# Two of the token norms of a three-layer kernel: one sum over tokens in place of eight, and the third weight unit worked beside the first two

## The chip, the cores and the metric

One core of one Trainium2 chip. The metric is the device time of one execution, in microseconds (us); lower is better. The kernel is one program that runs three transformer layers one after another.

## The reference, cut to what matters

There are 512 tokens (`SEQ`) of width 1024 (`D_MODEL`), in float32. Every sublayer adds a normed result to the residual, and the next sublayer takes a normed copy of that residual:

```python
def rmsnorm(x, gain):
    x32 = x.astype(jnp.float32)
    y = x32 * lax.rsqrt(jnp.mean(x32 * x32, axis=-1, keepdims=True) + RMS_EPS)
    return (y * gain.astype(jnp.float32)).astype(x.dtype)

        h = memory_cross_attention(rmsnorm(x, norm_cross_pre[l]), rmsnorm(mem, mem_norm[l]), ...)
        x = x + rmsnorm(h, norm_cross_post[l])
        h = conv_glu_ffn(rmsnorm(x, norm_ffn_pre[l]), w_ffn_in[l], ffn_conv_w[l], ffn_conv_b[l], w_ffn_out[l])
        x = x + rmsnorm(h, norm_ffn_post[l])

def conv_glu_ffn(xn, w_up, conv_w, conv_b, w_down):
    gu = xn @ w_up
    gate, up = jnp.split(gu, 2, axis=-1)
    gate = causal_dwconv(gate, conv_w) + conv_b.astype(gate.dtype)
    return (jax.nn.silu(gate) * up) @ w_down
```

At two places a post-norm, an addition to `x` and a pre-norm stand back to back: after the cross attention (`norm_cross_post`, then `norm_ffn_pre` ahead of the gated FFN), and after that FFN (`norm_ffn_post`, then `attn_norm_e_2` ahead of the projections of the next layer's attention). These are the double norms of this case.

## The kernel before, in words

**Layout.** Activations lie feature-major: 1024 features are 8 blocks (`KT`) of 128 partitions, with 512 tokens along the free axis. A weight *unit* is a 128x1024 slice of a weight matrix: all 8 feature blocks for 128 output features. All 339 units of the kernel are one stream in `w_in`.

**Products in three passes.** Each float32 operand is split into a high and a low part (`wh`, `wl`; `xh`, `xl`), and a product is `wh*xh + wh*xl + wl*xh`. So one unit costs TensorE (PE) 8 blocks x 3 = 24 matmuls of 128x512, which add up in one PSUM bank.

**The weight ring.** Four buffers (`RING`). SyncE (SP) loads unit k into `raw` once unit k-4 is done (`unit_done`); ScalarE (ACT) rounds it into `wh` in `raise_to`, in its own program order (`high_split`); GpSimd (POOL) then makes `wl = raw - wh` in `lower`, in two halves of 128x512 (`unit_split`). VectorE (DVE) takes finished PSUM banks away and counts them in `emptied`.

**A double norm.** The pre-norm's factor 1/rms of a token is applied to the *results* of the products, so PE can begin on `x*gain` before that factor is known. DVE (`normed_twice`) makes for each block b: `scale` (tmp = y*gain*factor, the factor read from PSUM), `accumulate` (x += tmp), and for the block before it `low` (xl = x*gain - xh). ACT (`prepare`) makes for each block xh = x*gain, and its square into one of two `sq` buffers, which it may fill again when PE has used it. PE (`early_units`) works two units (n0 and n0+1) side by side in this block loop: for block kt four high products (`wh*xh`, `wl*xh` of both units), and for the block before it `low_product`: first `token_sums` of its squares, then `wh*xl` of both units. `token_sums` sums the squares over features as 4 matmuls with 4 columns each, which the trace shows as 8. After the loop come units n0+2 and n0+3 whole (`piece`), into the two `score_ps` banks.

**What follows the sum.** ACT takes the square root (L1511), DVE the reciprocal (L2118), PE spreads it over the partitions (`spread_tokens`, 4 transposes, L758; after two blocks of n0+2), and DVE copies it into `rstd` (L2159). Only then can DVE empty unit n0 and the ones behind it.

**After the first double norm** (n0 = `fup0`), units come in pairs of gate (even) and up (odd) blocks. DVE's `gated` makes for a pair: the gate emptied and scaled (L2090), a convolution of three instructions (L2391, L2097), after ACT's SiLU the product with the up bank (L2610), the factor again (L2611) and the split into high and low (L2101, L2102). ACT's `gated` raises units up to n0+2i+4 ahead of the SiLU of pair i. Units n0+4 and n0+5 (`next_unit`) go to the `gemm_ps` banks of n0 and n0+1 once these are emptied; from n0+6 on (`units`) each unit waits until the unit two before it is emptied:

```python
                        for n in range(first, first + RING):
                            pe.wait_ge(unit_split, RING * i + (n + 1))
                            pe.wait_ge(emptied, RING * i + (n - 1))
```

**After the second double norm** (n0 = `even_in`), ACT waits until unit n0 is emptied, squares it for the head norms (L1976), and only then raises unit n0+4; PE does `query_stat(0)`, then `next_unit(n0+4)`.

Queues are strictly in program order on each engine. The order around the change is written out by hand; no planner sets it.

Of the kernel before, what the change touches and what calls it, by code (L numbers as in the profile page):

```python
# [31 lines left out]
D = 1024  # L32
KT = D // P
# [151 lines left out]
def build(nc, x_in, mem_in, w_in, par_in, con_in, moba_in, alibi_in, na_in, dist_in, out):  # L185
    with ExitStack() as ctx:
# [200 lines left out]
        def early_bank(n0, n):  # L387

            return score_ps[:, n - n0 - 2, :] if n - n0 in (2, 3) else gemm_ps[:, n % 2, :]
# [179 lines left out]
        def _(pe):  # L569
# [109 lines left out]
            def early_units(n0, highs):  # L679


                keep_clock(2)
                pe.wait_ge(unit_split, n0 + 2)
                pe.wait_ge(emptied, n0)
                both = [(n, early_bank(n0, n)) for n in (n0, n0 + 1)]

                def low_product(kt):
                    take(square_ready)
                    token_sums(sq[:, kt % 2, :], kt == 0, kt == KT - 1).then_inc(square_used, 1)
                    pe.wait_ge(rhs_ready, blocks_split[0] + kt + 1)  # L690
                    for n, o in both:
                        m = pe.matmul(o, wh[:, n % RING, kt * P:(kt + 1) * P], xl[:, kt, :], start=False,
                                      stop=(kt == KT - 1))
                        if kt == KT - 1:
                            m.then_inc(unit_done, 1)

                for kt in range(KT):
                    w = slice(kt * P, (kt + 1) * P)
                    pe.wait_ge(high_made, highs + kt + 1)
                    for n, o in both:  # L700
                        pe.matmul(o, wh[:, n % RING, w], xh[:, kt, :], start=(kt == 0), stop=False)
                        pe.matmul(o, wl[:, n % RING, w], xh[:, kt, :], start=False, stop=False)
                    if kt:
                        low_product(kt - 1)
                low_product(KT - 1)
                blocks_split[0] += KT
                for n in (n0 + 2, n0 + 3):
                    pe.wait_ge(unit_split, n + 1)
                    piece(n, early_bank(n0, n), 0, 2, xh, xl)
                    if n == n0 + 2:  # L710
                        spread_tokens()
                    piece(n, early_bank(n0, n), 2, KT, xh, xl)

            def next_unit(n, h, l):

# [756 lines left out]
        def _(act):  # L1472
# [17 lines left out]
            def raise_to(n):  # L1490

                while raised[0] <= min(n, UNITS - 1):
# [4 lines left out]
                    act.activation(wh[:, k % RING, :], raw[:, k % RING, :], ACT.Copy).then_inc(high_split, 1)  # L1497
                    raised[0] += 1

            def prepare(src, gain, h, ready=None, adds=0, tokens=False, banks={}):  # L1500


                base = taken.get(square_added, 0)
                act.activation(eps[:, 3:4], eps[:, 0:1], ACT.Sqrt)
                for b in range(KT):
                    high_and_square(src, gain, h, b, ready, base=base if adds else None, bank=banks.get(b))
                if adds:
                    taken[square_added] = base + adds
                if tokens:
                    take(square_used, 2)  # L1510
                    act.activation(token_std, turn_ps[:, 0, 0:T], ACT.Sqrt, bias=eps[:, 0:1],  # L1511
                                   scale=1.0 / D).then_inc(std_ready, 1)
                else:
                    finish_norm(rstd[:, :])
# [428 lines left out]
            def crossed(b):  # L1943
# [5 lines left out]
                else:  # L1949
# [2 lines left out]
            last = (FIRST["co"] + U_CO - 1) % 2  # L1952
            prepare(y, None, None, crossed, adds=KT - 3, tokens=True,
                    banks={KT - 2: score_ps[:, last, :], KT - 1: gemm_ps[:, last, :]})
            prepare(x, "norm_ffn_pre", xh, lambda b: take(block_ready), tokens=True)
            raise_to(FIRST["fup0"] + 3)
            gated()

            act.wait_ge(emptied, FIRST["fdown1"] + KT)
# [6 lines left out]
                    table_piece(arena[:, (23 + b) * N:(24 + b) * N], alibi_in[:, b * N:(b + 1) * N])  # L1966

            prepare(y, None, None, stored_and_loaded, adds=KT - 2, tokens=True)
            prepare(x, "attn_norm_e_2", xh, lambda b: take(block_ready), tokens=True)
            even, even_out = FIRST["even_in"], FIRST["even_out"]  # L1970
            raise_to(even + 3)
            for b in range(5):
                act.wait_ge(emptied, even + b + 1)
                if b >= 2:
# [94 lines left out]
        def _(dve):  # L2069
# [58 lines left out]
            def normed_twice(post, pre):  # L2128


                inverse_tokens()
                added = taken.get(block_ready, 0)
                made = []

                def scale(b):
                    if b >= 2:
                        dve.wait_ge(block_ready, added + b - 1)
                    sent_stt(tmp[:, b % 2, :], y[:, b, :], p_(post, b), spread_rstd, ALU.mult, ALU.mult)
                    made.append(taken[dve_step])

                def accumulate(b):
                    dve.wait_ge(dve_step, made[b])
                    sent(dve.tensor_tensor(x[:, b, :], x[:, b, :], tmp[:, b % 2, :], ALU.add), block_ready)

                scale(0)
                accumulate(0)
                scale(1)
                for b in range(1, KT):
                    if b + 1 < KT:
                        scale(b + 1)  # L2150
                    accumulate(b)
                    low(x, pre, xh, xl, b - 1)
                low(x, pre, xh, xl, KT - 1)
                inverse_spread()

            def inverse_spread():
# [806 lines left out]
```

## Time and profile before

| | |
|---|---|
| time, median of 3 runs | 2170.78 us (2170.11 to 2171.26) |
| span of the profiled execution (first to last instruction) | 2169.7 us |
| PE busy | 2149.4 us (99%), 10303 matmuls |
| DVE / ACT / POOL busy | 983.0 / 847.1 / 893.9 us (45 / 39 / 41%) |
| first double norm, from its first product to the end of unit n0+3 | 409.62 to 440.24 us of the span |
| second double norm, the same | 784.54 to 815.16 us |

The profiled execution has no device time of its own beside its span. The median of the runs is 1.1 us above that span, the work that lies around it. Times below are positions in the span. A matmul's own duration (some 390 ns) overlaps its neighbours' because the engine is pipelined; the distance from start to start is what it costs.

### The profile page before, as it was taken

The numbers are of one execution on the slowest core, as the hardware profiler recorded it, in microseconds if no ns is written. First come the engines' busy times: TensorE is split into PE (matmuls) and PEld (weight loads), VectorE is DVE, ScalarE is ACT, GpSimd is POOL, SyncE is SP. The second block draws the span as 40 slices with busy tenths as digits, with TensorE's granted clock in tenths as the row PEclk, the third lists the DMA queues.
The fourth block names the chain that finished last, engine by engine and source line by source line (L and its number), as shares of the span: only waits on it lengthen the run. The fifth ranks groups of instructions, "written<-read, shape, count | busy, mean of one in ns | idle before, by whom it ended". The sixth has DMA issues, their size and how long they took to land.

```text
span 2169.7 us, 27420 instructions
## 1 busy us (share of the span) xinstructions
PE 2149.4 (99%) x10303; PEld 1731.4 (80%) x10303; DVE 983.0 (45%) x1496; ACT 847.1 (39%) x1282; POOL 893.9 (41%) x684
## 2 busy tenths in 40 slices
PE   9999999999999999999999999999999999999999
PEld 7875787788888877767888888888888878888887
DVE  5755645576626143465432231346534655313221
ACT  6435645422222243565433232444333434423221
POOL 5431254154444443213444444433343315444443
PEclk9999999999999999999999999999999999999999
DMA  4222132133322332102222222322222213222223
GB/s 175 78 68 69 57 99 78 59 102 122 106 97 97 110 113 88 50 30 69 97 97 97 97 97 97 106 81 75 78 87 78 72 44 109 97 97 97 97 97 97
DMA packets 55109, 193.24 MB, mean 89 GB/s; under 512 B 6112, under 2 KB 6368, under 8 KB 54752
## 3 DMA queue, kind: packets, MB, share of 16 engines
q1 hardware_dynamic: 50112, 180.41, 25.0%
q10 hardware_dynamic: 4896, 11.41, 1.6%
q8 instruction: 73, 1.20, 0.2%
q14 instruction: 28, 0.23, 0.0%
HBM read 189.69 MB, written 2.10 MB: 88 GB/s over the span
## 4 chain that ended last, share of the span: by engine, by line
issue 52%; POOL 29%; PE 17%; POOLq 1%; DMA 0%; DVE 0%; ACT 0%; SPq 0%; ACTq 0%
POOL wl L552 29%; PE gemm_ps L587 6%; PE gemm_ps L588 6%; PE gemm_ps L589 6%; POOLq L549 0%; POOLq L561 0%; DMA x<-x_in 0%; DVE xl L2090 0%; ACT xh L1892 0%; ACT wh L1497 0%; PE turn_ps L729 0%; DVE x L2236 0%; SPq L526 0%; ACTq L1891 0%
## 5 line engine op out<-in xcount | busy, mean ns | idle before, releaser
L552 POOL TENSOR_TENSOR wl<-raw,wh 128x512 fp32r<-128x512 f32 x678 | 890.1, 1335 | 1258.0 <-ACT wh L1497 1248.8
L1497 ACT ACTIVATE wh<-raw 128x1024 fp32r<-128x1024 f32 x339 | 358.7, 1059 | 752.7 <-DMA raw<-w_in 742.1
L587 PE MATMUL gemm_ps<-xh,wh 128*128 128x512 f32 x1176 | 465.8, 396 | 0.0
L589 PE MATMUL gemm_ps<-xh,wl 128*128 128x512 f32 x1176 | 459.0, 390 | 0.0
L588 PE MATMUL gemm_ps<-xl,wh 128*128 128x512 f32 x1176 | 458.8, 390 | 0.0
L588 PE MATMUL gemm_ps<-arena_r,wh 128*128 128x512 f32 (+1 forms) x1088 | 417.0, 383 | 0.0
L587 PE MATMUL gemm_ps<-arena_r,wh 128*128 128x512 f32 (+1 forms) x832 | 320.0, 385 | 1.2 <-POOL wl L552 0.7
L589 PE MATMUL gemm_ps<-arena_r,wl 128*128 128x512 f32 (+1 forms) x832 | 317.4, 381 | 0.0
L587 PEld LDWEIGHTS gemm_ps<-xh,wh 128*128 128x128 f32 x1176 | 221.5, 188 | 49.6 <-issue 2.3
L588 PEld LDWEIGHTS gemm_ps<-xl,wh 128*128 128x128 f32 x1176 | 221.5, 188 | 47.4 <-issue 2.2
L589 PEld LDWEIGHTS gemm_ps<-xh,wl 128*128 128x128 f32 x1176 | 221.3, 188 | 46.7
L588 PEld LDWEIGHTS gemm_ps<-arena_r,wh 128*128 128x128 f32 x1088 | 205.0, 188 | 41.2 <-issue 1.4
L2090 DVE SCALAR_TENSOR_TENSOR arena<-gemm_ps,rstd 128x512 f32<-128x512 f32 (+1 forms) x116 | 84.7, 731 | 261.9 <-PE gemm_ps L589 211.1
L2236 DVE TENSOR_TENSOR x<-x,gemm_ps 128x512 f32<-128x512 f32 x84 | 57.6, 686 | 316.8 <-PE gemm_ps L589 305.1
L587 PEld LDWEIGHTS gemm_ps<-arena_r,wh 128*128 128x128 f32 x832 | 157.0, 189 | 33.7 <-issue 2.4
L589 PEld LDWEIGHTS gemm_ps<-arena_r,wl 128*128 128x128 f32 x832 | 156.9, 189 | 30.1
L2097 DVE SCALAR_TENSOR_TENSOR tmp<-gemm_ps,rstd 128x512 f32<-128x512 f32 x64 | 44.2, 691 | 207.9 <-PE gemm_ps L589 207.9
L587 PE MATMUL gemm_ps<-y_r,wh 128*128 128x512 f32 x256 | 100.0, 391 | 0.0
L589 PE MATMUL gemm_ps<-y_r,wl 128*128 128x512 f32 x256 | 99.6, 389 | 0.0
L2586 DVE TENSOR_TENSOR arena_r<-sq,arena_r 128x512 fp32r<-128x512 f32 x64 | 93.7, 1464 | 2.2
L621 PE MATMUL gemm_ps<-xh,wh 128*128 128x512 f32 x216 | 88.5, 410 | 1.3 <-DVE xl L2308 0.5
L623 PE MATMUL gemm_ps<-xh,wl 128*128 128x512 f32 x216 | 84.6, 392 | 0.0
(429 smaller groups left out, 2548.6 us busy)
## 6 DMA issues: line engine op xcount, KB each, us to landing
raw<-w_in SPq DMA_DIRECT2D x338, 512.0 KB, 3.4
arena<-na_in ACTq DMA_DIRECT2D x14, 256.0 KB, 2.7
out<-x ACTq DMA_DIRECT2D x8, 256.0 KB, 2.9
x<-x_in SPq DMA_DIRECT2D x6, 256.0 KB, 6.5
arena<-alibi_in ACTq DMA_DIRECT2D x6, 256.0 KB, 3.5
arena<-moba_in ACTq DMA_DIRECT2D x1, 1024.0 KB, 4.8
arena<-mem_in ACTq DMA_DIRECT2D x1, 1024.0 KB, 5.6
arena<-dist_in ACTq DMA_DIRECT2D x1, 896.0 KB, 4.5
```

The lines of the kernel that those rows point to most:

```text
L552: m = pool.tensor_tensor(wl[:, k, half], raw[:, k, half], wh[:, k, half].bitcast(F32), ALU.subtract)
L587: pe.matmul(o, wh[:, n % RING, w], h[:, kt, 0:width], start=(kt == 0), stop=False)
L588: pe.matmul(o, wh[:, n % RING, w], l[:, kt, 0:width], start=False, stop=False)
L589: last = pe.matmul(o, wl[:, n % RING, w], h[:, kt, 0:width], start=False, stop=(kt == nkt - 1))
L621: pe.matmul(o, wh[:, n % RING, w], h[:, kt, :], start=(kt == 0), stop=False)
L623: m = pe.matmul(o, wl[:, n % RING, w], h[:, kt, :], start=False, stop=(kt == KT - 1))
L1497: act.activation(wh[:, k % RING, :], raw[:, k % RING, :], ACT.Copy).then_inc(high_split, 1)
L2090: sent(dve.scalar_tensor_tensor(out=o, in0=a, scalar=scalar, in1=b, op0=op0, op1=op1), s)
L2097: done(dve.scalar_tensor_tensor(out=o, in0=a, scalar=scalar, in1=b, op0=op0, op1=op1), s)
L2236: sent(dve.tensor_tensor(x[:, e, :], x[:, e, :], bank(n0, e), ALU.add), emptied)
L2586: done(dve.tensor_tensor(l[:, b, :], sq[:, b % 2, :], h[:, b, :].bitcast(F32), ALU.subtract), rhs_ready)
```

## The change

- The eight `token_sums` of the block loop go. ACT writes the squares of the pre-norm into the 8 blocks of `y` (free by then), in the new `prepare_into`, without waiting for anyone to use them. DVE adds them up into `square_sum` in seven additions (`sum_square`), the first ahead of the last `low`, six behind it. PE makes one `whole_token_sums` from that.
- Unit n0+2 trails in the block loop: from kt = 2 on, its three products of block kt-2. What is left of it (two blocks) and unit n0+3 follow; the token sums stand after 3 blocks of n0+3, the spread after 6.
- ACT raises unit n0+3 before the block loop, not after the norm.

```diff
--- before.py
+++ after.py
@@ -685,8 +685,6 @@
                 both = [(n, early_bank(n0, n)) for n in (n0, n0 + 1)]
 
                 def low_product(kt):
-                    take(square_ready)
-                    token_sums(sq[:, kt % 2, :], kt == 0, kt == KT - 1).then_inc(square_used, 1)
                     pe.wait_ge(rhs_ready, blocks_split[0] + kt + 1)
                     for n, o in both:
                         m = pe.matmul(o, wh[:, n % RING, kt * P:(kt + 1) * P], xl[:, kt, :], start=False,
@@ -702,14 +700,20 @@
                         pe.matmul(o, wl[:, n % RING, w], xh[:, kt, :], start=False, stop=False)
                     if kt:
                         low_product(kt - 1)
+                    if kt == 2:
+                        pe.wait_ge(unit_split, n0 + 3)
+                    if kt >= 2:
+                        piece(n0 + 2, early_bank(n0, n0 + 2), kt - 2, kt - 1, xh, xl)
                 low_product(KT - 1)
                 blocks_split[0] += KT
-                for n in (n0 + 2, n0 + 3):
-                    pe.wait_ge(unit_split, n + 1)
-                    piece(n, early_bank(n0, n), 0, 2, xh, xl)
-                    if n == n0 + 2:
-                        spread_tokens()
-                    piece(n, early_bank(n0, n), 2, KT, xh, xl)
+                piece(n0 + 2, early_bank(n0, n0 + 2), KT - 2, KT, xh, xl)
+                pe.wait_ge(unit_split, n0 + 4)
+                piece(n0 + 3, early_bank(n0, n0 + 3), 0, 3, xh, xl)
+                whole_token_sums()
+                taken[square_made] = taken.get(square_made, 0) + KT
+                piece(n0 + 3, early_bank(n0, n0 + 3), 3, 6, xh, xl)
+                spread_tokens()
+                piece(n0 + 3, early_bank(n0, n0 + 3), 6, KT, xh, xl)
 
             def next_unit(n, h, l):
 
@@ -1496,6 +1500,19 @@
                         act.wait_ge(unit_done, k + 1 - RING)
                     act.activation(wh[:, k % RING, :], raw[:, k % RING, :], ACT.Copy).then_inc(high_split, 1)
                     raised[0] += 1
+
+            def prepare_into(gain, squares, n0):
+
+                act.activation(eps[:, 3:4], eps[:, 0:1], ACT.Sqrt)
+                raise_to(n0 + 3)
+                for b in range(KT):
+                    take(block_ready)
+                    act.activation(xh[:, b, :], x[:, b, :], ACT.Copy, scale=p_(gain, b)).then_inc(high_made, 1)
+                    act.activation(squares[:, b, :], x[:, b, :], ACT.Square).then_inc(square_made, 1)
+                taken[square_added] = taken.get(square_added, 0) + KT - 1
+                take(square_used, 2)
+                act.activation(token_std, turn_ps[:, 0, 0:T], ACT.Sqrt, bias=eps[:, 0:1],
+                               scale=1.0 / D).then_inc(std_ready, 1)
 
             def prepare(src, gain, h, ready=None, adds=0, tokens=False, banks={}):
 
@@ -1952,8 +1969,7 @@
             last = (FIRST["co"] + U_CO - 1) % 2
             prepare(y, None, None, crossed, adds=KT - 3, tokens=True,
                     banks={KT - 2: score_ps[:, last, :], KT - 1: gemm_ps[:, last, :]})
-            prepare(x, "norm_ffn_pre", xh, lambda b: take(block_ready), tokens=True)
-            raise_to(FIRST["fup0"] + 3)
+            prepare_into("norm_ffn_pre", y, FIRST["fup0"])
             gated()
 
             act.wait_ge(emptied, FIRST["fdown1"] + KT)
@@ -1966,9 +1982,8 @@
                     table_piece(arena[:, (23 + b) * N:(24 + b) * N], alibi_in[:, b * N:(b + 1) * N])
 
             prepare(y, None, None, stored_and_loaded, adds=KT - 2, tokens=True)
-            prepare(x, "attn_norm_e_2", xh, lambda b: take(block_ready), tokens=True)
+            prepare_into("attn_norm_e_2", y, FIRST["even_in"])
             even, even_out = FIRST["even_in"], FIRST["even_out"]
-            raise_to(even + 3)
             for b in range(5):
                 act.wait_ge(emptied, even + b + 1)
                 if b >= 2:
@@ -2142,6 +2157,13 @@
                     dve.wait_ge(dve_step, made[b])
                     sent(dve.tensor_tensor(x[:, b, :], x[:, b, :], tmp[:, b % 2, :], ALU.add), block_ready)
 
+                def sum_square(b):
+                    take(square_made, 2 if b == 1 else 1)
+                    if b > 1:
+                        landed(square_added)
+                    sent(dve.tensor_tensor(square_sum, y[:, 0, :] if b == 1 else square_sum, y[:, b, :], ALU.add),
+                         square_added)
+
                 scale(0)
                 accumulate(0)
                 scale(1)
@@ -2150,7 +2172,10 @@
                         scale(b + 1)
                     accumulate(b)
                     low(x, pre, xh, xl, b - 1)
+                sum_square(1)
                 low(x, pre, xh, xl, KT - 1)
+                for b in range(2, KT):
+                    sum_square(b)
                 inverse_spread()
 
             def inverse_spread():
```

## Rows read from the trace of the kernel before

**Rows 1.** The page, busy time of each engine.
```profile
PE 2149.4 (99%) x10303; PEld 1731.4 (80%) x10303; DVE 983.0 (45%) x1496; ACT 847.1 (39%) x1282; POOL 893.9 (41%) x684
```

**Rows 2.** Timeline of PE, first double norm: start us, us, instruction, count.
```profile
414.76 0.95 PE L740 MATMUL turn_ps<-con,sq 128*128 128x4 f32 x8
415.56 0.71 PE L692 MATMUL gemm_ps<-xl,wh 128*128 128x512 f32 x2
...
417.02 0.95 PE L740 MATMUL turn_ps<-con,sq 128*128 128x4 f32 x8
...
430.24 0.60 PE L758 MATMUL turn_ps<-con,eps 128*128 128x128 f32 x4
...
440.24 0.39 PE L621 MATMUL gemm_ps<-xh,wh 128*128 128x512 f32 x1
...
451.12 0.50 PE L587 MATMUL gemm_ps<-xh,wh 128*128 128x512 f32 x1
```

**Rows 3.** Timeline of DVE after the first double norm.
```profile
430.95 0.69 DVE L2159 COPY rstd<-turn_ps 128x512 f32<-128x512 f32 x1 [2.00 <-PE turn_ps L758]
...
433.18 2.45 DVE L2097 SCALAR_TENSOR_TENSOR tmp<-arena,par,tmp 128x512 f32<-128x512 f32 x2
436.48 0.69 DVE L2610 TENSOR_TENSOR tmp<-sq,gemm_ps 128x512 f32<-128x512 f32 x1 [0.85 <-ACT sq L1878]
...
450.37 0.69 DVE L2090 SCALAR_TENSOR_TENSOR arena<-gemm_ps,rstd 128x512 f32<-128x512 f32 x1
...
469.88 1.54 DVE L2097 SCALAR_TENSOR_TENSOR tmp<-arena,par,tmp 128x512 f32<-128x512 f32 x2
```

**Rows 4.** Timeline of ACT and of DVE in the first block loop, and DVE adding squares before it.
```profile
412.59 0.72 ACT L1520 ACTIVATE xh<-x,par 128x512 fp32r<-128x512 f32 x1 [0.68 <-DVE x L2143]
...
399.92 1.49 DVE L2212 TENSOR_TENSOR tmp<-tmp,sq 128x512 f32<-128x512 f32 x2 [0.70 <-ACT sq L1527]
...
409.95 0.68 DVE L2143 TENSOR_TENSOR x<-x,tmp 128x512 f32<-128x512 f32 x1
...
411.88 0.68 DVE L2143 TENSOR_TENSOR x<-x,tmp 128x512 f32<-128x512 f32 x1
...
420.84 0.68 DVE L2143 TENSOR_TENSOR x<-x,tmp 128x512 f32<-128x512 f32 x1
```

**Rows 5.** The page's DMA issues: count, size, us to landing.
```profile
raw<-w_in SPq DMA_DIRECT2D x338, 512.0 KB, 3.4
```

**Rows 6.** DVE and POOL at once: timelines, and one line's durations (min/median/max ns).
```profile
472.64 2.54 POOL L552 TENSOR_TENSOR wl<-raw,wh 128x512 fp32r<-128x512 f32 x2 [3.08 <-ACT wh L1497]
...
474.03 1.70 DVE L2611 TENSOR_TENSOR tmp<-tmp,rstd 128x512 f32<-128x512 f32 x1
...
L2090 DVE SCALAR_TENSOR_TENSOR xl<-x,par,xh x48: 737/751/1785, 7.2 to 1818.9; 128x512 fp32r<-128x512 f32 x48
```

**Rows 7.** Timelines of PE, DVE, ACT, POOL, second double norm.
```profile
805.16 0.60 PE L758 MATMUL turn_ps<-con,eps 128*128 128x128 f32 x4
...
815.96 0.49 PE L621 MATMUL gemm_ps<-xh,wh 128*128 128x512 f32 x1
...
805.87 0.69 DVE L2159 COPY rstd<-turn_ps 128x512 f32<-128x512 f32 x1 [2.00 <-PE turn_ps L758]
...
807.32 0.63 ACT L1976 ACTIVATE sq<-arena 128x512 f32<-128x512 f32 x1 [2.71 <-DVE arena L2090]
...
807.86 1.04 ACT L1497 ACTIVATE wh<-raw 128x1024 fp32r<-128x1024 f32 x1
...
808.98 5.04 POOL L552 TENSOR_TENSOR wl<-raw,wh 128x512 fp32r<-128x512 f32 x4 [1.76 <-ACT wh L1497]
```

**Rows 8.** Windows ahead of the second norm: us, PE, PEld, DVE, ACT, POOL busy, PEclk, DMA.
```profile
780.00:782.00 2.00, 1.36 (x8) 1.28 (x8) 0.18 (x1) 0.35 (x2) 1.01 (x1) 0.70 0.31 125
782.00:784.00 2.00, 2.00 (x4) 0.86 (x3) 1.80 (x3) 0.33 (x1) 0.00 (x0) 0.50 0.00 0
784.00:786.00 2.00, 1.84 (x6) 0.75 (x4) 2.00 (x4) 1.32 (x3) 0.00 (x0) 0.95 0.00 0
```

## The prediction, made before the changed kernel ran

> **What bounds the kernel now.** I read the page first: PE is busy for 2149.4 of 2169.7 us [rows 1]. So what PE is spared shortens the kernel, unless something else is late at that place. Averages don't tell that, so I followed each engine's timeline from each double norm until PE stands on its own again.
>
> In the block loop the reader is to see PE's step: from token sums to token sums 2.26 us [rows 2], for six products and one set of sums. Further on the 48 products of units n0+4 and n0+5 take from 440.24 to 451.12 [rows 2], 10.88 us, 0.227 us each. So 6 x 0.227 = 1.36 us are products and 0.90 us are the sums. DVE delivers a block of `x` every 1.93 us (409.95, 411.88 [rows 4]).
>
> Behind the loop, see how close DVE is. PE begins unit n0+6 at 451.12 [rows 2]. That unit needs the bank of n0+4, which DVE frees at 450.37 + 0.69 = 451.06 [rows 3]. The slack is 0.06 us. DVE gets there by a chain that begins where `rstd` is copied: from 431.64 (430.95 + 0.69) to 451.06 are 19.42 us [rows 3], nearly without a pause, through two pairs of the gated FFN. So time that PE is spared before 451 in the first norm can't be kept; only an earlier `rstd` would help. In the second norm a shorter chain binds in the same way: `rstd` copied at 806.56, unit n0 emptied and squared at 807.32, wh of n0+4 at 807.86, its wl from 808.98, 5.04 us for two units, so the first at 811.50; PE asks for it at 815.96 [rows 7]. Slack 4.5 us.
>
> **The sums, and the third unit in the loop.** Seven of eight sets go: 7 x 0.90 = 6.3 us less PE work in each norm. The third unit adds no work, it only moves. But the sums of blocks 0 and 1 also filled a wait: xh of block 2 is ready at 412.59 + 0.72 = 413.31 [rows 4], and PE, without the sums, is through with block 1 and low product 0 about 0.5 us before it can start. From block 2 on PE has 9 products, 2.04 us, against DVE's 1.93, and doesn't wait. Net 5.8 us less PE work in each norm, 11.6 us in all.
>
> **Where the spread goes.** Before it stand 48 + 6 products and 8 sets of sums; now 48 + 24 (all of n0+2) + 18 (six blocks of n0+3) = 90 and one set. 36 x 0.227 = 8.2 us later, 6.3 earlier, 0.5 wait: the spread, and `rstd` behind it, comes 2.4 us later, at 432.6 and 807.5 (430.24 [rows 2], 805.16 [rows 7]).
>
> **The additions on DVE.** Chained additions of squares are 0.75 us each (two in 1.49 [rows 4]). The first delays the last `low` by 0.7 us, which PE doesn't notice (it comes to it some 2 us later). Last accumulate ends at 421.5 [rows 4]; low, addition, low, six additions: 0.66 + 0.66 + 0.66 + 6 x 0.75, so 428.0. PE asks at 429.7. Cost nothing; if DVE were slowed by over 1.7 us it would pass on the rest. ACT has 1.3 us of work for a block against 1.93, and loses only waits.
>
> **Raising n0+3 before the loop.** Its load goes out when the unit before n0 is done and lands 3.4 us later [rows 5]; ACT needs 1.04 us for it [rows 7] and is free until xh of block 0, so ACT loses nothing. But POOL, idle in the loop before, now lowers it (2.54 us) just when DVE makes blocks 0 and 1. What that does is seen at 474.03: a DVE addition with both operands in SBUF took 1.70 us beside POOL (at work from 472.64 to 475.18), where additions of that shape alone take 0.68; the split `low` ranges from 0.74 to 1.79 [rows 4, 6]. `scale` reads PSUM and kept 0.69 in such rows (L2610, L2090 [rows 3]). Cost: from 0 to 2.1 us for two such meetings; I take 1.3 in the first norm, one half of POOL's work in front of `low` 0 and so of every later block, and 0.9 in the second, in front of the first accumulate. From block 2 PE starts as DVE allows, so this goes on to `rstd` whole.
>
> The Trainium skill ("SBUF — State Buffer", section "SBUF: two separate sides") says that the two engines share a port pair as an exclusive lock, taken by a DVE instruction with two SBUF inputs, and that the loser is blocked for the whole instruction. By it the sum keeps both charges; without it they would be nothing and the time 2.2 us less. The trace agrees: 474.03 to 475.73 ends 0.55 us after POOL's half does at 475.18 [rows 6].
>
> **Sum, first norm.** `rstd` 2.4 + 1.3 = 3.7 us later. Then the 19.42 us chain again. POOL's work of n0+4 falls ahead of the first convolution and frees it (2.45 us at 433.18 against 1.54 at 469.88 [rows 3]), but n0+5 and n0+6 then fall on the splits and the next convolution; bounds -0.9 and +0.9, I take +0.4. So n0+6 starts 4.1 us later than 451.12, at 455.2. PE waits for it: `rstd` is there at 435.3, n0 emptied 1 us later, so n0+4 runs from 436.3; n0+5 waits for its wl, raised behind the first SiLU, to about 442.7, and is done 5.44 us later at 448.2. That leaves 7 us idle. Behind it PE's 10.88 us for a pair exceed DVE's 9.4 (18.7 us from 431.64 to 450.37 for two [rows 3]), so there is no second wait, and nothing is given back.
>
> **The clock.** Before the second norm PE waits and does thin sums, and the granted clock goes from full to half: 0.70, 0.50, 0.95 in three windows of 2 us [rows 8], that is 1.2 + 2.0 + 0.2 = 3.4 us at the lower level (1.2 GHz), in which dense products would lose half, 1.7 us. The idle of 7 us ahead of n0+6 is longer than all of that stretch's waits together. I take one such dip: +1.7. Bounds 0 and 3.4. First norm: +5.8.
>
> **Sum, second norm.** The chain ends 2.4 us later: 811.5 + 2.4 = 813.9 against 815.96, so n0+4 starts 2.0 us earlier, not 5.8; less 0.9 of POOL: -1.1. PE idles some 3.7 us there; a dip is possible, I leave it to the range. What follows is bound by PE and stays as it is.
>
> Together +4.7 us: 2170.8 + 4.7 = 2175.5 (the profiled execution 2169.7 + 4.7 = 2174.4). On this kernel 0.2% (4.3 us) is about what a measurement can tell from no change; the forecast lies just over it.
>
> **The rivals.**
> (a) *DVE and POOL don't meet badly, and the clock holds.* For it: the median of the 48 splits is 0.75 us [rows 6], so most meetings cost nothing; against it 474.03. Then 2.4 + 0.4 - 2.0 = +0.8, and with one of the two costs up to +3.9: 2171.6 to 2174.7, no change.
> (b) *The clock falls in both norms, or two dips follow in the first.* +1.7 to +3.4 more: 2177.2 to 2179. For it: the idle in the second norm.
> (c) *PE is the bound, and its 11.6 us are gained:* 2159.2. It needs the DVE chain behind the first `rstd` to be 6 us or more shorter, or `rstd` to come earlier; it decides as soon as n0+6 starts before 451.12. For it only that PE is 99% busy; the 0.06 us of slack speaks against it.
> (d) *Half of that:* DVE catches up in the first norm (its two pairs include SiLU's table load and contention), the second gains its 2: 2168 to 2170.
>
> **How the numbers follow.** Forecast with both costs and one dip 0.41 (2174 to 2177), (a) 0.29, (b) 0.15, (c) 0.06, (d) 0.09. The range 2170.0 to 2179.5 leaves out (c), part of (d) and little of (b). Slower by over 4.3 us: most of the forecast (0.29) and (b): 0.44. Faster by as much: (c) and a rest, 0.08. Within: 0.48.
>
> **What would show it.** In the first norm: no sums in the loop, PE steps of about 2.04 us; the spread some 3.7 us later than 430.24; the row of unit n0+6 preceded by PE idle of 5 to 7 us released by DVE's L2090 of unit n0+4; a window at under 1.00 behind it. In the second: PE idle released by ACT's square and then by POOL, n0+4 at about 814.9 plus what the first norm cost. Additions to `x` over 1 us at blocks 0 or 1 show the port; at 0.68 all through, rival (a). Wrong if PE doesn't wait at n0+6.

## The result, and the profile after

The changed kernel takes 2172.82 us (median of 22 runs) against 2170.05 us of the kernel before beside it (22 runs). The ratio is 1.0019, with a 95% interval from 1.0012 to 1.0025, or +4.1 us (+2.6 to +5.4). One of the 22 runs of the changed kernel, 3052 us at a granted clock of 0.65, is in a slower state and isn't in the ratio. The forecast was +4.7 us.

The page of the kernel after, to be held against [rows 1]:

```profile
span 2168.1 us, 27222 instructions
PE 2138.2 (99%) x10191; PEld 1718.3 (79%) x10191; DVE 993.0 (46%) x1510; ACT 846.2 (39%) x1282; POOL 895.8 (41%) x684
```

PE has 112 matmul records and 11.2 us less to do (2138.2 for 2149.4), DVE 14 instructions and 10 us more. PE's saving appears in the busy time and not in the device time. The span needs care: it is 1.6 us *shorter* than before's 2169.7, though 22 runs say that the kernel is slower. The difference stands in code that nobody touched. Two windows of 50 us ahead of the first double norm, before and then after (columns as in [rows 8]):

```profile
200.00:250.00 50.00, 49.92 (x264) 36.78 (x262) 32.84 (x79) 28.67 (x58) 13.97 (x10) 0.93 0.22 74
...
300.00:350.00 50.00, 49.43 (x302) 42.84 (x301) 32.43 (x37) 24.52 (x34) 32.50 (x23) 0.97 0.35 115
```
```profile
200.00:250.00 50.00, 49.35 (x280) 36.12 (x280) 36.84 (x86) 30.30 (x64) 14.09 (x10) 1.00 0.22 74
...
300.00:350.00 50.00, 49.43 (x310) 42.53 (x309) 34.36 (x38) 25.55 (x38) 32.99 (x23) 1.00 0.35 116
```

The last but two column is the granted clock. In the profile of before it fell twice (0.93, 0.97), in that of after it didn't. So the first token sums of the first double norm (t0) stand at 403.18 us before and at 398.13 after: 5 us of chance, more than the whole effect. From here on I compare stretches that begin at t0, and at the same sums of the second norm (t1). In us:

| kernel (one profile each) | t0 | `rstd` copied, from t0 | n0+6 begins, from t0 | t0 to t1 | t1 to the end | t0 to the end |
|---|---|---|---|---|---|---|
| before | 403.18 | 28.46 | 47.94 | 374.47 | 1392.05 | 1766.5 |
| before again (e1) | 400.95 | 28.93 | 48.41 | 374.94 | 1391.71 | 1766.7 |
| after | 398.13 | 32.03 | 50.50 | 378.41 | 1391.56 | 1770.0 |

From t0 on, after is 3.3 to 3.5 us longer, which agrees with the ratio. All of it, 3.5 to 3.9 us, lies between t0 and t1, in the first norm and the units behind it. Behind t1 it is 0.15 to 0.5 us shorter, which is less than profiles of the same code differ by there (see the control).

**First norm after.** Timeline of DVE, POOL and PE, in order of time:

```profile
398.13 0.95 PE L744 MATMUL turn_ps<-con,tmp 128*128 128x4 f32 x8
...
402.94 0.75 DVE L2105 SCALAR_TENSOR_TENSOR tmp<-y_all,par,turn_ps 128x512 f32<-128x512 f32 x1 [1.29 <-PE turn_ps L762]
403.07 2.95 POOL L552 TENSOR_TENSOR wl<-raw,wh 128x512 fp32r<-128x512 f32 x2 [2.82 <-ACT wh L1501]
403.72 1.16 DVE L2158 TENSOR_TENSOR x<-x,tmp 128x512 f32<-128x512 f32 x1
406.12 0.68 DVE L2158 TENSOR_TENSOR x<-x,tmp 128x512 f32<-128x512 f32 x1
...
413.76 0.39 PE L699 MATMUL gemm_ps<-xh,wh 128*128 128x512 f32 x1
...
415.80 0.39 PE L699 MATMUL gemm_ps<-xh,wh 128*128 128x512 f32 x1
...
419.53 4.66 DVE L2164 TENSOR_TENSOR tmp<-tmp,y_all 128x512 f32<-128x512 f32 x6
...
425.77 0.95 PE L744 MATMUL turn_ps<-con,tmp 128*128 128x4 f32 x8
...
428.76 0.60 PE L762 MATMUL turn_ps<-con,eps 128*128 128x128 f32 x4
429.47 0.69 DVE L2184 COPY rstd<-turn_ps 128x512 f32<-128x512 f32 x1 [2.23 <-PE turn_ps L762]
...
431.70 1.54 DVE L2112 SCALAR_TENSOR_TENSOR tmp<-arena,par,tmp 128x512 f32<-128x512 f32 x2
...
438.11 0.50 PE L621 MATMUL gemm_ps<-xh,wh 128*128 128x512 f32 x1 [1.10 <-POOL wl L552]
...
447.88 0.69 DVE L2105 SCALAR_TENSOR_TENSOR arena<-gemm_ps,rstd 128x512 f32<-128x512 f32 x1
448.63 0.79 PE L587 MATMUL gemm_ps<-xh,wh 128*128 128x512 f32 x1 [4.79 <-DVE arena L2105]
451.36 0.53 PE L587 MATMUL gemm_ps<-xh,wh 128*128 128x512 f32 x1
```

The reader is to see five things. Without the sums a step of the loop is 2.04 us (413.76 to 415.80). The six additions are done at 424.19, 1.6 us before PE asks. The first `accumulate` takes 1.16 us beside POOL, the next one 0.68. The copy into `rstd` starts 31.34 us behind t0; before it was 27.77 (403.18, and 430.95 [rows 3]). And the first product of n0+6 bears in brackets an idle time of 4.79 us, ended by DVE emptying n0+4; its row before bears none (451.12 [rows 2]). It is the longest wait of PE in the kernel, and a new one.

**What follows it.** Windows of after, behind the wait and in the second norm:

```profile
446.00:448.00 2.00, 0.00 (x0) 0.00 (x0) 1.93 (x3) 0.00 (x0) 2.00 (x2) 1.00 0.33 133
448.00:450.00 2.00, 1.37 (x3) 1.16 (x4) 1.93 (x3) 0.00 (x0) 2.00 (x2) 0.55 0.00 0
450.00:452.00 2.00, 2.00 (x7) 1.55 (x6) 1.70 (x2) 0.23 (x1) 0.40 (x1) 0.59 0.00 0
452.00:454.00 2.00, 2.00 (x11) 1.65 (x10) 1.38 (x2) 1.44 (x2) 0.48 (x1) 1.00 0.04 8
...
814.00:816.00 2.00, 2.00 (x6) 1.53 (x5) 0.00 (x0) 0.00 (x0) 2.00 (x3) 0.50 0.12 39
```

The clock falls to its lower level (1.2 GHz) as n0+6 begins. Its first six products take 2.73 us (448.63 to 451.36) where six at the full clock take 1.36. From n0+6 to t1 the stretch is 327.91 us, before it was 326.53: 1.38 more. So the wait is paid in n0+6's start (+2.56 from t0), and the clock behind it once more (+1.38): +3.94 together. The second figure is firm: from n0+6 to t1 before, e1, e3, e10, e11 and e13, in which the clock held behind n0+6's start, have 326.5 to 326.6 us. Of the first, 0.74 us is chance, as the part on the prediction shows.

**Second norm after**, timeline, answering to [rows 7]:

```profile
776.54 0.95 PE L744 MATMUL turn_ps<-con,tmp 128*128 128x4 f32 x8
...
781.84 1.42 DVE L2158 TENSOR_TENSOR x<-x,tmp 128x512 f32<-128x512 f32 x1
...
807.83 0.69 DVE L2184 COPY rstd<-turn_ps 128x512 f32<-128x512 f32 x1 [2.23 <-PE turn_ps L762]
809.96 1.05 PE L657 MATMUL turn_ps<-con,sq 128*128 128x2 f32 x8 [0.84 <-ACT sq L1991]
813.49 0.80 PE L621 MATMUL gemm_ps<-xh,wh 128*128 128x512 f32 x1 [2.47 <-POOL wl L552]
```

The new waits are those named ahead, 0.84 us for ACT's square and 2.47 us for POOL. Unit n0+4 begins 36.95 us behind t1; before, 38.31: 1.36 sooner. But the clock fell here too (0.50 at 814 to 816), and by the time n0+4 is emptied nothing is left (44.31 us behind t1, before 44.10). That fall isn't chance: it stands behind the same two waits in all six profiles that have the changed second norm with the late spread (after, e3, e4, e6, e7, e13), and in none with the second norm as before.

### The profile page after: what moved, and what is told of

Same layout as the page of the kernel before. It is cut to its first block, busy times and chain, and to the rows that moved or that the text cites. A ratio compares the mean times of both kernels' runs of the same rounds, so it can differ in the third digit from the quotient of the medians.

```text
span 2168.1 us, 27222 instructions
## 1 busy us (share of the span) xinstructions
PE 2138.2 (99%) x10191; PEld 1718.3 (79%) x10191; DVE 993.0 (46%) x1510; ACT 846.2 (39%) x1282; POOL 895.8 (41%) x684
## 4 chain that ended last, share of the span: by engine, by line
issue 52%; POOL 29%; PE 17%; POOLq 1%; DMA 0%; DVE 0%; ACT 0%; SPq 0%; ACTq 0%
POOL wl L552 29%; PE gemm_ps L587 6%; PE gemm_ps L588 6%; PE gemm_ps L589 6%; POOLq L549 0%; POOLq L561 0%; DMA x<-x_in 0%; DVE xl L2105 0%; ACT xh L1909 0%; ACT wh L1501 0%; PE turn_ps L733 0%; DVE x L2261 0%; SPq L526 0%; ACTq L1908 0%
```

## The experiments

All ratios are against the kernel before on the same chip. Where the edit says `keep_clock(n)`, the kernel does n float32 products more than the reference needs, into a bank that nobody reads then, and nothing else differs in what is computed. Offsets from t0 and t1 are from one profile each; the table at the end of this section has them.

**The control (e1).** The kernel before, unchanged.

> The kernel before once more, as a control. Every theory: ratio 1.000, within 0.1% or so; its trace tells how much of the difference between the two profiles seen so far (the changed one comes to the first double norm 5.0 us earlier, in code that the change doesn't touch) is the change's. If that lead is chance, this trace lies anywhere between; the stretch from the first sums of the first norm to unit n0+6 is 47.9 us again, and n0+6 begins without a wait.

Ratio 1.0000 [0.9989, 1.0011]. Its t0 lies 2.2 us off before's, the stretch from t0 to the end within 0.15 us, and its two parts within 0.5. The table below has a wider check. Over the three profiles whose first norm is as before (before, e1, e3) the stretch from t0 to t1 is 374.47 to 375.53 us, and over the three whose second norm is as before (before, e1, e2) the one from t1 to the end is 1391.01 to 1392.05. So a difference of less than about 1 us between single profiles tells nothing.

**One norm alone (e2, e3).** Both forms of the functions stand in the kernel, and one norm calls the old ones:

```diff
 e2, second norm as before          e3, first norm as before
-early_units(even, 4 * KT)          -early_units(fup0, 3 * KT)
+early_units_before(even, 4 * KT)   +early_units_before(fup0, 3 * KT)
 ... and so for prepare_into and normed_twice
```

> The change at the first double norm alone, the second as before. Theory A (rstd late, the DVE chain of the gated FFN binds, then a clock dip): all of the loss is here, +2.6 us to unit n0+6 and +1.3 to +1.7 of the dip behind it, 2174 us (+3.9 to +4.3, ratio 1.0018 to 1.0020). Rival B (the loss is spread over both norms, or lies in DVE and POOL meeting): about +2 us. Rival C (PE bound): 5.8 us faster.

> The change at the second double norm alone. Theory A: unit n0+4 begins 1.4 us earlier, and a clock dip of 1.3 to 1.7 us behind its wait takes that back: 0.0 +- 0.5 us. Without a dip in a run, -1.4. Rival B (loss in both): +2. Rival C (PE bound): -5.8.

e2 took 1.0014 [1.0003, 1.0025], e3 0.9995 [0.9986, 1.0005]. The profiles say the same: e2 has t0 to t1 3.9 to 4.4 us longer. e3 has 0.6 to 1.1 longer there, in a first norm that is as before, and 0.6 to 1.0 shorter behind t1, but so has e2, whose second norm is as before; both are scatter. A nearer mark behind the second norm is the first transpose of `y_all`. It stands 82.2 to 82.3 us behind t1 in before, e1 and e2, and 82.1 to 83.3 in the six profiles with the changed second norm and the late spread. The loss is in the first norm, and the second gains nothing that shows.

**POOL moved out of the block loop (e4).** Unit n0+3 is raised behind the loop:

```diff
-                raise_to(n0 + 3)
                 for b in range(KT):
...
+                raise_to(n0 + 3)
                 taken[square_added] = taken.get(square_added, 0) + KT - 1
```

> The changed kernel, but ACT raises unit n0+3 behind the block loop, so that POOL is idle while DVE makes blocks 0 and 1. Theory A: first accumulates at 0.68 us in both norms (1.16 and 1.42 in the changed kernel); n0+6 of the first norm 0.5 us earlier, n0+4 of the second 0.7 us earlier, so 1.2 us less than the changed kernel, if the wl of n0+3, now made from about 20 us behind the loop's start, is there when PE asks for it 2 us later than that. Rival B (the meeting of the two engines is the main loss): 3 us less or more.

Ratio 1.0010 [1.0001, 1.0019], from t0 to the end 0.7 us less than after, where 1.2 was expected. From the first `scale` to n0+6 it has 45.58 us, after 45.69, e2 45.91: the 0.5 us expected there didn't come. Timeline of e4:

```profile
423.14 6.47 DVE L2164 TENSOR_TENSOR tmp<-tmp,y_all 128x512 f32<-128x512 f32 x6
423.60 3.07 POOL L552 TENSOR_TENSOR wl<-raw,wh 128x512 fp32r<-128x512 f32 x2 [18.70 <-ACT wh L1501]
```

The meeting with `accumulate` is gone, but POOL now meets the six additions: 6.47 us for 4.66. They end at 429.61, and PE, whose last product before the sums started at 429.15 (one starts every 0.227 us), begins the sums only at 429.67, 0.3 us late. In both places tried so far POOL's work met DVE instructions with two SBUF inputs; e10 puts it behind the additions. Rival B, 3 us or more from the meeting of the two engines, isn't borne out.

**The spread earlier (e5).** In the piece of n0+3:

```diff
-                piece(n0 + 3, early_bank(n0, n0 + 3), 0, 3, xh, xl)
+                piece(n0 + 3, early_bank(n0, n0 + 3), 0, 1, xh, xl)
                 whole_token_sums()
...
-                piece(n0 + 3, early_bank(n0, n0 + 3), 3, 6, xh, xl)
+                piece(n0 + 3, early_bank(n0, n0 + 3), 1, 3, xh, xl)
                 spread_tokens()
```

> The changed kernel with the token sums after one block of unit n0+3 (three in the change) and the spread after three (six). The products, additions and raises are those of the change. Theory A (what counts is when rstd is there): rstd 2.0 us earlier in both norms; the wait ahead of n0+6 in the first norm falls from 4.8 to some 2.8 us and brings no clock dip, n0+4 in the second starts 2.0 us earlier, without a dip: against the kernel before +0.6 in the first norm and -3.3 in the second, 2.7 us faster (ratio 0.9988), against the changed kernel 6 us. Rival C (PE work counts, order doesn't): as the changed kernel, ratio 1.0015.

Ratio 0.9997 [0.9988, 1.0006]; t0 to the end 4.1 us less than after. `rstd` comes 2.0 us sooner (29.99 for 32.03). The larger part came from the second norm: 1388.20 us from t1 to the end against 1391.56, and the first transpose of `y_all` stands 78.8 us behind t1 for 82.5. In the first the idle stayed at 4.79 us, where some 2.8 without a dip were expected, and with it the dip. Timeline of PE, then the window, of e5:

```profile
452.18 0.80 PE L587 MATMUL gemm_ps<-xh,wh 128*128 128x512 f32 x1 [4.79 <-DVE arena L2105]
```
```profile
452.00:454.00 2.00, 1.82 (x4) 1.50 (x5) 1.93 (x3) 0.00 (x0) 1.94 (x2) 0.50 0.00 0
```

That is what the dependence demands. PE's n0+5 waits for POOL (by 1.10 us in after, 0.54 here), and POOL for a raise that ACT makes behind the first SiLU, so an earlier `rstd` starts both DVE's chain and PE's n0+5 sooner: from n0+5 to n0+6 are 10.52 us in after and 10.54 in e5.

**The wait filled (e6, e13).** PE does unread products ahead of n0+6:

```diff
+            keep_clock(10)        # e13: keep_clock(5)
             units(fup0 + 6, 2 * FF1_PARTS[0] - 6, xh, xl)
```

> The changed kernel with ten products that nobody reads (some 0.4 us each) in PE's wait ahead of unit n0+6 of the first norm. Theory A: n0+6 begins at the same distance from the norm's first sums (50.5 us), the granted clock stays at 1.00 behind it, and 1.3 to 2.0 us are saved against the changed kernel. If there is no cost in the clock, nothing changes; if PE's wait isn't a wait but work, it gets 4 us slower.

> The changed kernel with five unread float32 products (4.3 us) ahead of n0+6 of the first norm, in a wait of 4.8 us; the run with ten put 8.5 us there. Theory A: n0+6 stays 50.5 us from the norm's first sums, no window below 1.00 behind it, 1.3 to 2.0 us less than the changed kernel: 2171 us (ratio 1.0008 to 1.0012). Without a cost in the clock: ratio 1.0017 as the changed kernel.

e6: 1.0023 [1.0014, 1.0033]. e13: 1.0011 [1.0002, 1.0020]. Timeline of PE, e6 and then e13:

```profile
443.80 8.74 PE L677 MATMUL out_ps<-con 128*128 128x512 f32 x20
451.98 0.79 PE L587 MATMUL gemm_ps<-xh,wh 128*128 128x512 f32 x1
```
```profile
449.04 4.45 PE L677 MATMUL out_ps<-con 128*128 128x512 f32 x10
454.00 0.50 PE L587 MATMUL gemm_ps<-xh,wh 128*128 128x512 f32 x1 [0.51 <-DVE arena L2106]
```

In e6 I sized the filler wrongly: ten such products take over 8 us (8.74 with the end of the last), so n0+6 came 3.2 us later (53.72 for 50.50). With five, an idle of 0.51 us is left and n0+6 starts at a clock that doesn't fall: from there to t1 326.54 us, before 326.53, after 327.91. That isolates the second price: 1.4 us of the loss is the clock behind the wait, and the wait itself stays. (n0+6 came at 51.16 us and not at 50.5, since POOL held the first `accumulate` for 1.76 us in this execution.)

**Other banks for n0+4 and n0+5 (e7).** They go to two banks of `out_ps`, so that n0+6 needs only n0 emptied and n0+7 only n0+1. The first unit that waits for DVE's later work is n0+8, which needs n0+6 emptied:

```diff
+            if n0 == FIRST["fup0"] and n - n0 in (4, 5):
+                return out_ps[:, n - n0 - 4, :]
...
+            for n in (fup0 + 6, fup0 + 7):
+                pe.wait_ge(unit_split, n + 1)
+                pe.wait_ge(emptied, n - 5)
+                piece(n, gemm_ps[:, n % 2, :], 0, KT, xh, xl)
+            units(fup0 + 8, 2 * FF1_PARTS[0] - 8, xh, xl)
```

> The changed kernel, but units n0+4 and n0+5 of the first norm go to two other PSUM banks (out_ps), so that n0+6 needs only n0 emptied, n0+7 only n0+1, and the first that waits for DVE is n0+8 (for n0+6). Theory A (the chain on DVE, not the banks, sets the pace): the wait moves to n0+8, which starts when DVE has emptied n0+6, 27.7 us behind rstd: 59.8 us from the first sums, against 61.4 in the changed kernel, plus the dip if it comes: 1 to 2.5 us faster than the changed kernel, no more. Rival D (only the two banks bind): all 5.8 us of PE's first norm are gained, and 1.3 of the dip: 6 us faster than the changed kernel.

Ratio 1.0012 [1.0003, 1.0021]. Timeline and window of e7:

```profile
403.39 1.80 DVE L2165 TENSOR_TENSOR x<-x,tmp 128x512 f32<-128x512 f32 x1
406.09 0.47 PE L701 MATMUL gemm_ps<-xh,wh 128*128 128x512 f32 x1 [1.88 <-ACT xh L1517]
...
460.48 0.50 PE L589 MATMUL gemm_ps<-xh,wh 128*128 128x512 f32 x1 [3.25 <-DVE arena L2112]
```
```profile
408.00:410.00 2.00, 2.00 (x5) 1.62 (x6) 2.00 (x4) 1.32 (x3) 0.00 (x0) 0.50 0.00 0
...
462.00:464.00 2.00, 2.00 (x6) 1.52 (x6) 1.55 (x2) 0.38 (x1) 0.25 (x1) 0.50 0.00 0
```

The wait went from n0+6 to n0+8 (3.25 us), and the clock fell behind it too. From `rstd` to n0+8 it was 27.81 us, so it is DVE's pace over the pairs behind `rstd` that PE meets, not the lack of two banks. In this execution the collision also came out worse: `accumulate` 1.80 us, PE 1.88 us idle ahead of the loop, and the clock fell *inside* the loop, so `rstd` came 34.13 us behind t0 and n0+8 at 61.94, where 59.8 was expected.

**The sums alone (e8).** No trailing; n0+2 and n0+3 whole behind the loop as before, but one whole sum, after 6 blocks of n0+2, and the spread after all 8:

```diff
-                    if kt >= 2:
-                        piece(n0 + 2, early_bank(n0, n0 + 2), kt - 2, kt - 1, xh, xl)
...
+                piece(n0 + 2, early_bank(n0, n0 + 2), 0, 6, xh, xl)
                 whole_token_sums()
+                piece(n0 + 2, early_bank(n0, n0 + 2), 6, KT, xh, xl)
                 spread_tokens()
+                piece(n0 + 3, early_bank(n0, n0 + 3), 0, KT, xh, xl)
```

> The changed kernel without its second half: unit n0+2 doesn't trail in the block loop but follows it; the sums stand after six blocks of n0+2 and the spread after eight, so that rstd comes as early as in the run with the early spread. PE idles in the block loop some 0.6 us for each block. Theory A: both norms as with the early spread within 1 us, since the chain from rstd binds, so 2 to 3 us faster than before; the trailing unit buys nothing. Rival C (PE work counts): 3.4 us slower for each norm than the run with the early spread.

Ratio 0.9983 [0.9974, 0.9992]: faster than before. From t0 to the end it has 1766.1 us, e5 1765.9. So what counts is when the spread comes, and the trailing unit buys nothing by itself. The timed ratios of e5 and e8 differ more than the two profiles; their intervals overlap, and I leave that open. In both the whole gain stands behind t1. Ahead of it they have 377.7 and 378.0 us, still some 3 more than before, for the wait at n0+6 (2.99 us in e8) and the dip are still there.

**The raise behind the additions (e10), with a filler (e11), with the banks (e12).** On top of e8, ACT waits for six of the seven additions before it raises n0+3 behind the loop:

```diff
+                act.wait_ge(square_added, taken.get(square_added, 0) + KT - 2)
+                raise_to(n0 + 3)
 e11: + keep_clock(3) ahead of n0+6
 e12: + the banks of e7, and ahead of n0+8:
+            pe.wait_ge(emptied, fup0 + 6)
+            keep_clock(2)
```

> The run with the sums alone (unit n0+2 behind the loop, sums after six of its blocks), and ACT raises unit n0+3 when six of the seven additions are made, so that POOL lowers it after DVE's last addition and before PE asks for it. Theory A: no accumulate over 0.7 us, rstd 0.4 to 0.7 us earlier in each norm, hence 0.8 to 1.4 us less than the sums alone, 2165 us (ratio 0.9978). Rival: the wl of n0+3 is late for PE; that costs nothing in the first norm, where the DVE chain binds, and up to 0.5 us in the second.

> The same with three unread float32 products (two trace rows of 0.43 us each, 2.6 us together) in PE's wait ahead of unit n0+6 of the first norm, which is 3.0 us. Theory A: n0+6 begins where it did, the clock stays at 1.00 behind it, and 1.5 to 2.5 us are saved against the same kernel without them, 2163 us (ratio 0.9968). If the clock costs nothing, no difference; if the wait is shorter than 2.6 us, the difference is lost again.

> The same as the timed raise, with units n0+4 and n0+5 of the first norm in two other PSUM banks and two unread products ahead of n0+8. Theory A: n0+8 starts 27.8 us behind rstd, 57.3 us from the norm's first sums, where the kernel before has 58.8: 1.5 us less than with the timed raise and without a dip, 2163 us. Rival D (banks alone bind): PE runs through, 3 us or more less.

| kernel | ratio, 95% interval | median | `rstd` copied, from t0 | n0+6 begins, from t0 | t0 to t1 | t1 to the end | t0 to the end |
|---|---|---|---|---|---|---|---|
| e2 | 1.0014 [1.0003, 1.0025] | 2172.64 | 31.97 | 50.44 | 378.86 | 1391.01 | 1769.9 |
| e3 | 0.9995 [0.9986, 1.0005] | 2168.70 | 29.48 | 48.96 | 375.53 | 1391.08 | 1766.6 |
| e4 | 1.0010 [1.0001, 1.0019] | 2173.14 | 31.18 | 49.65 | 377.80 | 1391.44 | 1769.2 |
| e5 | 0.9997 [0.9988, 1.0006] | 2169.99 | 29.99 | 49.14 | 377.66 | 1388.20 | 1765.9 |
| e6 | 1.0023 [1.0014, 1.0033] | 2174.86 | 32.02 | 53.72 | 380.57 | 1392.27 | 1772.8 |
| e13 | 1.0011 [1.0002, 1.0020] | 2171.40 | 32.67 | 51.16 | 377.70 | 1391.86 | 1769.6 |
| e7 | 1.0012 [1.0003, 1.0021] | 2172.04 | 34.13 | | 379.22 | 1392.04 | 1771.3 |
| e8 | 0.9983 [0.9974, 0.9992] | 2166.11 | 30.17 | 48.71 | 377.95 | 1388.13 | 1766.1 |
| e10 | 0.9995 [0.9985, 1.0004] | 2167.10 | 28.98 | 47.56 | 374.11 | 1387.58 | 1761.7 |
| e11 | 0.9983 [0.9973, 0.9993] | 2166.60 | 29.58 | 48.20 | 374.73 | 1387.33 | 1762.1 |
| e12 | 0.9968 [0.9956, 0.9981] | 2162.97 | 29.71 | | 373.26 | 1387.14 | 1760.4 |

Timeline of e10: `accumulate` free of POOL, POOL's four halves in one block behind the additions, and a wait of 3.03 us ahead of n0+6, here without a dip.

```profile
407.96 0.69 DVE L2155 TENSOR_TENSOR x<-x,tmp 128x512 f32<-128x512 f32 x1
...
428.33 5.04 POOL L552 TENSOR_TENSOR wl<-raw,wh 128x512 fp32r<-128x512 f32 x4 [23.22 <-ACT wh L1497]
...
450.67 0.50 PE L587 MATMUL gemm_ps<-xh,wh 128*128 128x512 f32 x1 [3.03 <-DVE arena L2102]
```

By its profile e10 should be 4.4 us faster than e8; the timed runs show no difference from before (expected was a ratio of 0.9978). One profile is one execution, and this one had no dip; whether others had one isn't shown, and it stays open. e11 and e12 have the same stretches as e10 within 1.3 us, and their times agree with them better, though e11 too missed its forecast (0.9983 for 0.9968); its interval overlaps that of e10, so what the filler alone brings isn't shown by the times. In e12, timeline of PE, the filler ends as n0+8 begins, so that nothing is idle at the place of the wait:

```profile
459.78 1.88 PE L679 MATMUL out_ps<-con 128*128 128x512 f32 x4
461.41 0.50 PE L589 MATMUL gemm_ps<-xh,wh 128*128 128x512 f32 x1
```

e12 is the fastest: 0.9968, some 6.9 us less than before and 11 less than after. It keeps the one part of the change that pays (one sum for eight), puts the spread earlier, POOL's work behind the additions, and PE's wait two units later. Of the 11.6 us that PE is spared it gets 6 to 7. By the profile 1.2 to 1.7 of them stand between t0 and t1 and 4.6 to 4.9 behind t1: the saving is kept in the second norm, where the slack was, and hardly in the first. Its two steps beyond e10 (banks, filler) weren't timed apart, and it was timed in only 6 runs.

## Why the prediction was right, point by point

- **DVE's chain binds at n0+6, and PE's saving isn't kept.** Right: the wait of 4.79 us stands there, and e7 shows that it follows DVE's pace. Loop steps of 2.04 us, as forecast. Rival (c), 2159.2, needed this to be otherwise.
- **The additions are free.** Right, with the cover forecast (1.6 us measured, 1.7 forecast); e4 shows what happens when that cover is used up.
- **Spread and `rstd` 2.4 us later by the order.** Right: from the first `scale` to the spread 25.82 us (402.94 to 428.76), before 22.99, and 0.48 of the 2.83 are the collision: 2.35 us. e5 takes 2.0 of it back and with both norms costs nothing against before.
- **POOL's collision.** The mechanism is right, the size in the first norm was not: 0.48 us (1.16 for 0.68) where I took 1.3. The mistake is the step "one half of POOL's work in front of `low` 0": DVE's `accumulate` ended at 404.88 and POOL's two halves at 406.02, so DVE got in between them. In the second norm it was 0.74 (1.42 for 0.68) where I took 0.9. Over all profiles that raise n0+3 ahead of the loop there are 14 such meetings, and the addition took 1.10 to 1.80 us in them: a cost of 0.4 to 1.1 us, 0.8 on average. So 0.9 was well sized, 1.3 was above all of them, and after's 0.48 was a mild case. The Trainium skill ("SBUF — State Buffer", section "SBUF: two separate sides") describes the loser as blocked while the other's instruction lasts; the rows fit that, and on both sides, since POOL's pair took 2.95 us instead of 2.54.
- **`rstd` 3.7 us later.** Measured 3.57: 2.35 of order, 0.48 of collision, and 0.74 that I had not forecast, from the sums ahead of the norm to the first `scale` (4.81 us for 4.07). That distance is 4.07 to 4.91 us over the 14 profiles and doesn't follow the kernel: e4, e7 and e13 have 4.07 with the changed norm, e3 4.67 with the old one. So the 0.74 is chance. That the sum of 3.7 was hit is luck, since it made up for the small collision.
- **The chain from `rstd` to n0+6, +0.4.** Wrong sign: 18.47 us for 19.48, -1.0. The convolution that took 2.45 us [rows 3] took 1.54 with POOL's work gone, as I had seen. The price that I set against it, POOL on the splits and on the next convolution, didn't come, because POOL stood beside them in the kernel before as well: the step that failed is counting that as new. This is the largest error of the sum. The two splits and the next convolution of before, then of after:

```profile
437.93 1.40 DVE L2101 CAST arena_r<-tmp 128x512 fp32r<-128x512 f32 x1
439.36 1.67 DVE L2102 TENSOR_TENSOR arena_r<-tmp,arena_r 128x512 fp32r<-128x512 f32 x1
442.50 2.45 DVE L2097 SCALAR_TENSOR_TENSOR tmp<-arena,par,tmp 128x512 f32<-128x512 f32 x2
```
```profile
435.53 1.40 DVE L2116 CAST arena_r<-tmp 128x512 fp32r<-128x512 f32 x1
436.97 1.64 DVE L2117 TENSOR_TENSOR arena_r<-tmp,arena_r 128x512 fp32r<-128x512 f32 x1
440.07 2.44 DVE L2112 SCALAR_TENSOR_TENSOR tmp<-arena,par,tmp 128x512 f32<-128x512 f32 x2
```

- **n0+6 4.1 us later, PE idle 7.** 2.56 later, idle 4.79. In before's frame n0+5 ended at 448.9 (forecast 448.2) and n0+6 began at 453.7 (455.2); 0.7 and 1.5 are the 2.2 us that are missing.
- **One dip, 1.7.** In the first norm 1.38 by the stretch, 1.4 by e13, which has the wait and no dip. And, as forecast, no part of either was given back behind it.
- **First norm +5.8**: +3.94 (2.56 + 1.38), or 3.2 without the chance of 0.74; e2 has 3.9 by the same count.
- **Second norm -1.1**: n0+4 did begin 1.36 us sooner, behind the two waits forecast (3.3 us against 3.7). But the dip that I had left to the range came and used it up: the difference behind t1 is within the scatter, and at the first transpose of `y_all` it is 82.5 us for 82.2. The term is nothing where I had -1.1. That the clock falls in both norms was the condition of rival (b), and it came true; its 2177.2 did not, because the first norm cost less than forecast.
- **Sum +4.7**: +3.3 to +3.5 in the profiles, +4.1 by the runs. The errors of the first norm (-1.9) and of the second (about +1.1) partly cancelled, so the total is better than its terms, and that part is luck.

In the second norm the prediction said that n0+4 would gain 2.0 us of its 5.8, since `rstd` comes later and the slack is used up. e5 and e8 bear that out from the other side: with the spread earlier they gain 3.4 us behind t1 against after. In e5 `rstd` is copied 2.1 us sooner there (29.87 us behind t1 for 31.98) and n0+4 begins 2.1 us sooner (34.84 for 36.95), so there too each microsecond of `rstd` counts once the sums are gone from PE. The rest goes with the clock, which didn't fall there.

## What to carry to other kernels

Before you take work from the busiest engine, find the next place where it waits for another's chain and measure the slack there: here 0.06 us, and a saving of 5.8 us in front of it bought nothing until that chain itself began sooner. A statistic's reader should be placed by the product count in front of it, not by the loop that it came from. Moved 36 products back, 8.2 us, it lost more than the 6.3 us of the seven sums. Compare stretches between two common points instead of the spans of two profiles, when the clock makes spans vary by more than the effect.

## What the runs showed of the hardware that I had not expected

- **The clock behind a wait in dense work.** The granted clock fell behind the wait of 4.8 us ahead of n0+6 in four profiles of four that had it (after, e2, e4, e5). Behind shorter waits: at n0+6 it fell behind 3.0 us in e8, whose row stands below, and not in e10; at n0+8 it fell behind 3.25 us (e7); in the second norm it fell in six profiles of six behind waits of 0.84 and 2.47 us with thin sums between them, and not behind 1.55 us (e5). With unread products in the wait (e6, e11, e13) it didn't fall. Each fall at n0+6 cost 1.4 to 2.7 us more, beside a wait of 4.8 or 3.0 us.

```profile
450.53 0.80 PE L587 MATMUL gemm_ps<-xh,wh 128*128 128x512 f32 x1 [2.99 <-DVE arena L2101]
```

- **Chance in untouched code.** t0 lay between 398.1 and 403.8 us over 14 profiles, with granted clocks of 0.93 to 1.00 in 200:250 and 0.97 to 1.00 in 300:350. The two go together: the four profiles with 1.00 in both have t0 at 398.1 to 398.5, the six with 0.93 and 0.97 at 402.8 to 403.8, the other four between. What makes the clock fall in one execution and not in the next isn't shown.
- **A plain float32 product of 128x512 costs about 0.86 us**: ten of them are 20 rows in the trace of e6, each of 0.59 us, in 8.74 us together, so a row follows every 0.43 us. One pass of the three costs 0.227.
